# Output projections that finish their token blocks one after another in the last column group

## The chip, the core and the metric

The kernel runs on one core of one Trainium2 chip. The metric is the device time of one execution in microseconds (us), as the median of several executions. A profiled execution also leaves a trace, from which all rows below are taken.

## The reference

The reference is a chain of four transformer-like layers on 256 tokens of width 1024 (plus 256 context tokens in layer 0), all in fp32. What matters here is the same in all four: a mixer (attention in layers 0 and 1, a gated scan in the last two), its output projection into the residual stream through a gate, and a norm that needs whole rows of the updated stream:

```python
x = x + g1 * (mix @ w_out)                 # mix: tokens x 1024, w_out: 1024 x 1024
h = rmsnorm(x, norm2_w) * (1 + sc2) + sh2  # mean of squares over the 1024 columns
x = x + g2 * swiglu(h, ...)                # last layer: eight experts instead
```

Layer 0 does this for 512 tokens (its context rows have a gate of their own), the others for 256.

## The kernel before

The four output projections are calls of `split_linear` (line 746), named `l0_w_out`, `l1_w_out`, and `w_out` for scan layers 0 and 1. They are those calls of it that are given `gates`; each is also given `residual`. The input projections use the same function without either.

The columns of the product are cut into groups (`cols`): two of 512 for an output projection. The tokens are cut into blocks of 128: four in layer 0, two elsewhere. `units[i]` lists the blocks of group i, and each block of a group has its own PSUM bank of 512 fp32 columns. An fp32 product is made of three TensorE products of halves: high by high, high by low, low by high (lines 806, 807, 808). The contraction of 1024 is cut into eight steps k. The order before is: group, then k, then block, so all banks of a group are completed together, in the last k.

The weights of a group come in four pieces of two k each. ScalarE makes the high half of a piece (line 825), VectorE the low half (`lows`, line 844). After the last product of a piece TensorE adds one to `piece_used`. VectorE waits for two pieces of a group and releases the ring slot of its first half, then for all four, releases the second slot, and only then stores the blocks. Each engine runs its own list in order. SyncE's list (`feed`, lines 310 and 316) waits for a released slot and starts the load of the item four places further on in the plan. In the plan an output projection's four half groups are followed by three `ada` items and the first feed-forward weights, in the last layer by the expert weights (`moe`) at once.

A store is two VectorE operations (lines 883 and 884, in layer 0 lines 1718 and 1719): the bank times the gate row into a scratch tile, then the addition to the residual tile. After each store ScalarE squares the new stretch of 512 columns and sums it (`part_square`, line 526).

`with nc.Block()` ends with a barrier of all engines. The next block is `modulate` (line 547): VectorE makes the reciprocal root from the sums (lines 531 and 513 to 518), the two engines normalise the rows (lines 597 and 658), and TensorE meanwhile does one `ada` product (line 420, not in the last layer), spreads gate rows (line 537) and then turns the normalised rows (line 633). The feed-forward block or the router comes after it.

Of the kernel before, what the change touches and what calls it, by code (L numbers as in the profile page):

```python
# [28 lines left out]
KD = D // PB  # L29
# [56 lines left out]
class Signal:  # L86


    def __init__(self, nc, ctx, name):
        self.sem = ctx.enter_context(nc.semaphore(name))  # L90
        self.base = 0
# [14 lines left out]
class Signals:  # L106


    def __init__(self, sig):
        self.ready = sig("ready")  # L110
        self.turned = sig("turned")
        self.evacuated = sig("evacuated")
        self.made = sig("made")
        self.scored = sig("scored")
        self.maxed = sig("maxed")
        self.expd = sig("expd")
        self.p_turned = sig("p_turned")
        self.p_copied = sig("p_copied")
        self.summed = sig("summed")
        self.scaled = sig("scaled")  # L120
        self.kq_turned = sig("kq_turned")
        self.kq_kept = sig("kq_kept")
        self.weighted = sig("probs_weighted")
        self.out_kept = sig("out_kept")
        self.up_done = sig("up_done")
        self.silu_done = sig("silu_done")
        self.act_done = sig("act_done")
        self.hop_a = sig("hop_a")
        self.hop_b = sig("hop_b")
        self.hop_c = sig("hop_c")  # L130
        self.hop_d = sig("hop_d")
        self.down_done = sig("down_done")
        self.hi_gu = sig("hi_gate_up")
        self.hi_d = sig("hi_down")
        self.prod = sig("product_made")
        self.act_hi = sig("hidden_hi")
        self.ada_rows = sig("ada_rows")
        self.ada_kept = sig("ada_kept")
        self.ada_cols = sig("ada_cols")
        self.ada_out = sig("ada_out")  # L140
        self.gate_made = sig("gate_row_made")
        self.gate_kept = sig("gate_row_kept")
        self.ht_kept = sig("turned_kept")
        self.tok_turned, self.tok_hi, self.tok_lo = sig("tokens_turned"), sig("tokens_hi"), sig("tokens_lo")
        self.got_hi, self.got_lo = sig("gathered_hi"), sig("gathered_lo")
        self.hi_kept, self.lo_kept = sig("gathered_hi_kept"), sig("gathered_lo_kept")
        self.lo_kept_act, self.picked = sig("gathered_lo_kept_act"), sig("tokens_picked")
        self.put_turned, self.put_kept = sig("put_turned"), sig("put_kept")
        self.spread, self.spread_kept = sig("gates_spread"), sig("gates_spread_kept")
        self.ht_odd, self.scales = sig("turned_odd_kept"), sig("modulation_scales")  # L150
        self.bank_done, self.tail_added = sig("ffn_bank_done"), sig("ffn_tail_added")
        self.w_hi, self.w_lo = sig("weight_hi"), sig("weight_lo")
        self.h_hi, self.h_lo = sig("input_hi"), sig("input_lo")
        self.piece_used = sig("weight_piece_used")


class MixSignals:
# [55 lines left out]
def build(nc, ctx, d, out):  # L213
# [34 lines left out]
    PS = ctx.enter_context(nc.psum_tensor("ps", [PB, 8, 512], F32))  # L248
# [10 lines left out]
    def sig(name):  # L259
        return Signal(nc, ctx, name)  # L260
# [9 lines left out]
    S = Signals(sig)  # L270
# [100 lines left out]
    def release(eng):  # L371
        eng.sem_inc(front_used.sem, 1)
        eng.sem_inc(back_used.sem, 1)
# [372 lines left out]
    def split_linear(toks, h_hi, h_lo, room, cols, blocks, store, src=None, beside=None, gates=(), nb=0, turned=None,  # L746
# [4 lines left out]
        bank = lambda q: (q % banks + first) % 8  # L751
# [3 lines left out]
        units = [[(b, c0, w) for b in blocks(c0)] for c0, w in cols]  # L755
        starts = [sum(len(u) for u in units[:i]) for i in range(len(units) + 1)]
        total, most = len(units), max(w for _, w in cols)
# [10 lines left out]
        with nc.Block() as block:  # L768
            if beside is not None:
                @block.gpsimd  # L770
                def _(pool):
                    beside(pool)
# [5 lines left out]
            @block.tensor  # L778
            def _(pe):
                if not gates:  # L780
                    zero_products(pe, 8, 7)
                gate_products(pe, gates)
                for k in range(KD if nb else 0):
                    if turn_bank(k) < first:
                        pe.wait_ge(S.gate_kept.sem, S.gate_kept.at(turn_bank(k) // 2 + 1))
                    for b in range(nb):
                        t = pe.transpose(PS[:, turn_bank(k), b * PB:(b + 1) * PB], XN[:, b, k * PB:(k + 1) * PB], ident)
                    t.then_inc(S.turned.sem, 1)
                for i in range(total):
                    for q in range(starts[i], starts[i + 1]):  # L790
                        if q < 8 and bank(q) < first:
                            pe.wait_ge(S.gate_kept.sem, S.gate_kept.at(bank(q) // 2 + 1))
                    if starts[i + 1] > banks:
                        pe.wait_ge(S.evacuated.sem, S.evacuated.at(starts[i + 1] - banks))
                    w = wide(i)
                    for k in range(KD):
                        if k % 2 == 0:
                            pe.wait_ge(S.w_lo.sem, S.w_lo.at(i * per_group + k // 2 + 1))
                        if i == 0:
                            pe.wait_ge(S.h_lo.sem, S.h_lo.at(max(k + 1, len(units[0]) if nb else 0)))  # L800
                        hi = hi_piece(i, k // 2)[:, k % 2 * w:(k % 2 + 1) * w]
                        lo = raw(RINGR, i, k // 2)[:, k % 2 * w:(k % 2 + 1) * w]
                        for j, (b, c0, _) in enumerate(units[i]):
                            o = PS[:, bank(starts[i] + j), 0:w]
                            t = slice(b * PB, (b + 1) * PB)
                            pe.matmul(o, h_hi(k)[:, t], hi, start=(k == 0), stop=False)
                            pe.matmul(o, h_hi(k)[:, t], lo, start=False, stop=False)  # L807
                            mm = pe.matmul(o, h_lo(k)[:, t], hi, start=False, stop=(k == KD - 1))
                        if k % 2 == 1:
                            mm.then_inc(S.piece_used.sem, 1)  # L810
                    if turned and i == 2:
                        turned[0](pe)

# [22 lines left out]
            @block.vector  # L836
            def _(dve):
                def lows(i):
                    for p in range(per_group):
                        if i and p == 2:  # L840
                            dve.wait_ge(S.piece_used.sem, S.piece_used.at((i - 1) * per_group + 2))
                            release(dve)
                        dve.wait_ge(S.w_hi.sem, S.w_hi.at(i * per_group + p + 1))
                        dve.tensor_tensor(raw(RINGR, i, p), raw(flat, i, p), hi_piece(i, p).bitcast(F32),
                                          ALU.subtract).then_inc(S.w_lo.sem, 1)
                        for k in range(2 * p, 2 * p + 2) if i == 0 else ():
                            dve.wait_ge(S.h_hi.sem, S.h_hi.at(k + 1))
                            dve.tensor_tensor(h_lo(k), src(k), h_hi(k).bitcast(F32), ALU.subtract).then_inc(S.h_lo.sem, 1)

                lows(0)  # L850
                if gates:
                    dve.wait_ge(S.gate_kept.sem, S.gate_kept.at(len(gates)))
                for i in range(total):
                    if i + 1 < total:
                        lows(i + 1)
                    else:
                        dve.wait_ge(S.piece_used.sem, S.piece_used.at(i * per_group + 2))
                        release(dve)
                    dve.wait_ge(S.piece_used.sem, S.piece_used.at((i + 1) * per_group))
                    release(dve)  # L860
                    for j, (b, c0, w) in enumerate(units[i]):
                        store(dve, PS[:, bank(starts[i] + j), 0:w], b, c0, w).then_inc(S.evacuated.sem, 1)
        if nb:
            S.turned.done(KD)
        S.gate_made.done(len(gates))
# [8 lines left out]
    def zero_products(pe, n, bank):  # L874

        for _ in range(n):
            pe.matmul(PS[:, bank, :], Z16[:, 0:PB], Z16[:, :], start=True, stop=True)
# [837 lines left out]
    def store_both(dve, ps, b, c0, w):  # L1715
# [9 lines left out]
             gates=[(gate_row, 0, 5, 0), (ctx_gate, 0, 5, 1)])  # L1725
# [446 lines left out]
    for layer in range(2):  # L2172
# [20 lines left out]
        def keep_conv(act):  # L2193
            for j in range(3):
# [12 lines left out]
                 gates=[(gate_row, lay, 5, 2)])  # L2207
        if layer == 0:
# [5 lines left out]
        lg, ix, h1, h2, gates, sel, pos = (SM[:, 32 + 16 * i:48 + 16 * i].rearrange("p (b e) -> p b e", b=2)  # L2214
                                           for i in range(7))
# [380 lines left out]
```

## Time and profile before

| | |
|---|---|
| median of 3 executions | 2720.43 us (2712.69 to 2722.75) |
| the profiled execution | 2713.4 us |
| its span, first to last instruction | 2711.1 us |
| mean granted TensorE clock | 0.953 |
| TensorE matmuls, busy | 2462.7 us (91%) |
| VectorE, busy | 1890.3 us (70%) |
| ScalarE, busy | 1471.5 us (54%) |
| 16 DMA engines' share, mean rate | 674.35 MB at 249 GB/s |

The busy share is a mean over stages that have different limits: the last third of the span is the expert stage. The trace's timelines show each engine's instructions in order of time. A bracket behind a row holds the time that the engine was idle before it, and the instruction that ended the wait. A releaser named PEq L768 is the barrier at the end of a `split_linear` block.

### The profile page before, as it was taken

The page shows a single profiled execution, that of the slowest core. Times are in us where ns is not written, and L with a number is a line of the kernel's source. Part 1 is how long each engine was busy: PE and PEld are TensorE (multiplying, and loading weights), DVE is VectorE, ACT ScalarE, POOL GpSimd, SP SyncE. Part 2 cuts the span into 40 slices and gives each one's busy share as a digit, 9 for nine tenths or more (in the row PEclk, how much of TensorE's full clock was granted, in tenths as well). Part 3 has the DMA queues.
Part 4 walks back from the last instruction along what each step waited for, and adds up shares of the span by engine and source line. Part 5 has one row for each costly group of instructions (what it writes and reads, how often), then busy time and mean ns, then how long its engine had stood idle before and what let it go on. Part 6 is the DMA issues. An engine that isn't in the chain of part 4 may idle for free. (4 is left out here: it accounts for less than half of the span.)

```text
span 2711.1 us, 58120 instructions
## 1 busy us (share of the span) xinstructions
PE 2462.7 (91%) x22998; PEld 1860.1 (69%) x22998; DVE 1890.3 (70%) x2521; ACT 1471.5 (54%) x1865; POOL 14.9 (1%) x12
## 2 busy tenths in 40 slices
PE   6978899999897789999899999888999999999997
PEld 4646677677664457768667768666777777777775
DVE  3276555555645666655666555669999999999997
ACT  3146444433421545443444434348887888888885
POOL 0000000000200000000000000000000000000000
PEclk9989999999888989999799999789999999999999
DMA  7340555554466127545275545338999999999995
GB/s 297 120 191 24 212 203 206 210 200 156 148 227 243 62 99 257 196 177 208 110 260 198 208 157 206 111 138 335 417 414 401 418 418 418 418 408 418 418 416 228
DMA packets 121210, 674.35 MB, mean 249 GB/s; under 512 B 13488, under 2 KB 13968, under 8 KB 67088
## 3 DMA queue, kind: packets, MB, share of 16 engines
q1 hardware_dynamic: 120032, 664.47, 63.6%
q10 hardware_dynamic: 1072, 8.42, 0.9%
q8 instruction: 72, 1.18, 0.2%
q14 instruction: 34, 0.28, 0.0%
HBM read 671.79 MB, written 1.05 MB: 248 GB/s over the span
## 5 line engine op out<-in xcount | busy, mean ns | idle before, releaser
L942 PE MATMUL ps<-projected,normed_or_mix 128*128 128x256 bf16 x1504 | 409.9, 273 | 1.2 <-issue 1.2
L943 PE MATMUL ps<-projected,normed_or_mix 128*128 128x256 bf16 x1504 | 409.9, 273 | 0.0
L1328 DVE TENSOR_TENSOR aux<-weights,aux 128x1024 bf16<-128x1024 f32 x224 | 272.5, 1217 | 2.3 <-ACT aux L1272 2.3
L1323 DVE TENSOR_TENSOR normed_or_mix<-weights,normed_or_mix 128x2048 bf16<-128x2048 f32 x111 | 254.0, 2289 | 15.8 <-ACT normed_or_mix L1266 11.2
L1323 DVE TENSOR_TENSOR turned<-weights,turned 128x2048 bf16<-128x2048 f32 x112 | 256.3, 2289 | 7.3 <-ACT turned L1266 2.6
L1266 ACT ACTIVATE turned<-weights 128x2048 bf16<-128x2048 f32 x112 | 213.6, 1907 | 50.8 <-DMA weights<-moe 50.6
L1266 ACT ACTIVATE normed_or_mix<-weights 128x2048 bf16<-128x2048 f32 x111 | 211.8, 1908 | 49.0 <-DMA weights<-moe 46.2
L1196 PE MATMUL ps<-projected,normed_or_mix 128*128 (+1 forms) x1792 | 234.6, 207 | 3.3 <-DVEq L1353 3.3
L1272 ACT ACTIVATE aux<-weights 128x1024 bf16<-128x1024 f32 x224 | 233.2, 1041 | 3.8 <-PE ps L1210 3.5
L1198 PE MATMUL ps<-projected,normed_or_mix 128*128 (+1 forms) x1792 | 234.6, 207 | 0.0
L1197 PE MATMUL ps<-projected,normed_or_mix 128*128 (+1 forms) x1792 | 234.6, 207 | 0.0
L1196 PE MATMUL ps<-projected,turned 128*128 (+1 forms) x1792 | 233.0, 206 | 0.7 <-DVE turned L1323 0.7
L1198 PE MATMUL ps<-projected,turned 128*128 (+1 forms) x1792 | 233.0, 206 | 0.0
L1197 PE MATMUL ps<-projected,turned 128*128 (+1 forms) x1792 | 233.0, 206 | 0.0
L807 PE MATMUL ps<-weights_halves,normed_or_mix_halves 128*128 128x512 f32 (+4 forms) x576 | 218.6, 379 | 0.0
L1208 PE MATMUL ps<-aux,probs 128*96 128x512 bf16 x448 | 172.6, 385 | 45.9 <-DVE probs L1338 45.9
L944 PE MATMUL ps<-projected,aux 128*128 128x256 bf16 x752 | 205.0, 273 | 0.0
L944 PE MATMUL ps<-projected,normed_or_mix 128*128 128x256 bf16 x752 | 205.0, 273 | 0.0
L974 DVE TENSOR_TENSOR probs_turned<-probs,ps 128x256 f32<-128x256 f32 x94 | 39.6, 421 | 229.3 <-ACT probs L967 229.3
L967 ACT ACTIVATE probs<-ps 128x256 f32<-128x256 f32 x94 | 36.1, 384 | 295.3 <-PE ps L944 295.1
L1196 PEld LDWEIGHTS ps<-projected,normed_or_mix 128*128 128x128 bf16 x1792 | 176.0, 98 | 8.8 <-issue 3.7
L1197 PEld LDWEIGHTS ps<-projected,normed_or_mix 128*128 128x128 bf16 x1792 | 176.0, 98 | 6.5
(385 smaller groups left out, 5960.0 us busy)
## 6 DMA issues: line engine op xcount, KB each, us to landing
weights<-moe SPq DMA_DIRECT2D x224, 1024.0 KB, 8.5
weights<-moe SPq DMA_DIRECT2D x224, 512.0 KB, 6.6
weights<-l_ffn SPq DMA_DIRECT2D x66, 1024.0 KB, 5.1
weights<-ada SPq DMA_DIRECT2D x64, 1024.0 KB, 5.6
weights<-l_ffn SPq DMA_DIRECT2D x66, 512.0 KB, 5.5
weights<-ada SPq DMA_DIRECT2D x64, 512.0 KB, 6.2
weights<-ffn SPq DMA_DIRECT2D x28, 1024.0 KB, 5.2
weights<-w_in SPq DMA_DIRECT2D x24, 948.0 KB, 4.7
```

Source lines behind the costliest of these rows:

```text
L807: pe.matmul(o, h_hi(k)[:, t], lo, start=False, stop=False)
L942: pe.matmul(o, hi, h_hi(k), start=(k == 0), stop=False)
L943: pe.matmul(o, hi, h_lo(k), start=False, stop=False)
L944: mm = pe.matmul(o, lo, h_hi(k), start=False, stop=(k == KD - 1))
L1196: pe.matmul(o, hi[:, t], xh, start=(k == 0), stop=False)
L1197: pe.matmul(o, hi[:, t], xl, start=False, stop=False)
L1198: mm = pe.matmul(o, lo[:, t], xh, start=False, stop=(k == KD - 1))
L1208: pe.matmul(o, hi, w_hi[:, t], start=start, stop=False)
L1266: act.activation(gu4[j % SLOTS][0], RING[:, slot(j), 0:2 * D], ACT.Copy).then_inc(S.hi_gu.sem, 1)
L1272: act.activation(down4[j % SLOTS][0], RING[:, slot(j), 2 * D:3 * D], ACT.Copy).then_inc(S.hi_d.sem, 1)
L1323: dve.tensor_tensor(gu4[j % SLOTS][1], RING[:, slot(j), 0:2 * D], gu4[j % SLOTS][0], ALU.subtract).then_inc(front_used.sem, 1)
L1328: dve.tensor_tensor(down4[j % SLOTS][1], RING[:, slot(j), 2 * D:3 * D], down4[j % SLOTS][0], ALU.subtract).then_inc(back_used.sem, 1)
```

## The change

In the last column group of the calls with `gates`, the block becomes the outer loop and k the inner one: all 24 products of one block, then all 24 of the next. At the end of each block but the last, TensorE signals `block_made`. `piece_used` counts in this group only in the last block. VectorE stores all blocks but the last as their signals come, ahead of its two waits for pieces and its two releases of slots; the last block's store stands behind them, as before. ScalarE's list is not changed. No instruction that computes or loads is added or taken away.

```diff
+        self.block_made = sig("last_group_block")
...
-                    for k in range(KD):
-                        if k % 2 == 0:
+                    last = bool(gates) and i == total - 1
+                    for part, k in itertools.product(range(len(units[i]) if last else 1), range(KD)):
+                        if k % 2 == 0 and part == 0:
                             pe.wait_ge(S.w_lo.sem, S.w_lo.at(i * per_group + k // 2 + 1))
...
                         for j, (b, c0, _) in enumerate(units[i]):
+                            if last and j != part:
+                                continue
...
-                        if k % 2 == 1:
+                        if k % 2 == 1 and (not last or part == len(units[i]) - 1):
                             mm.then_inc(S.piece_used.sem, 1)
+                        elif last and k == KD - 1:
+                            mm.then_inc(S.block_made.sem, 1)
...
+                def keep_block(i, j):
+                    b, c0, w = units[i][j]
+                    store(dve, PS[:, bank(starts[i] + j), 0:w], b, c0, w).then_inc(S.evacuated.sem, 1)
...
                 for i in range(total):
+                    last = len(units[i]) - 1
+                    early = last if gates and i == total - 1 else 0
                     if i + 1 < total:
                         lows(i + 1)
                     else:
+                        for j in range(early):
+                            dve.wait_ge(S.block_made.sem, S.block_made.at(j + 1))
+                            keep_block(i, j)
                         dve.wait_ge(S.piece_used.sem, S.piece_used.at(i * per_group + 2))
                         release(dve)
                     dve.wait_ge(S.piece_used.sem, S.piece_used.at((i + 1) * per_group))
                     release(dve)
-                    for j, (b, c0, w) in enumerate(units[i]):
-                        store(dve, PS[:, bank(starts[i] + j), 0:w], b, c0, w).then_inc(S.evacuated.sem, 1)
+                    for j in range(early, last + 1):
+                        keep_block(i, j)
```

## Rows read from the trace of the kernel before

**Rows 1.** The page's rate of the DMA engines in 40 slices of the span.

```profile
GB/s 297 120 191 24 212 203 206 210 200 156 148 227 243 62 99 257 196 177 208 110 260 198 208 157 206 111 138 335 417 414 401 418 418 418 418 408 418 418 416 228
```

**Rows 2.** Timeline of TensorE, layer 0: start us, duration us, engine, line, operation.

```profile
280.05 0.39 PE L808 MATMUL ps<-projected_halves,turned_halves 128*128 128x512 f32 x1
280.27 0.39 PE L806 MATMUL ps<-projected_halves,normed_or_mix_halves 128*128 128x512 f32 x1
...
280.73 0.39 PE L808 MATMUL ps<-projected_halves,turned_halves 128*128 128x512 f32 x1
...
292.97 0.39 PE L808 MATMUL ps<-projected_halves,turned_halves 128*128 128x512 f32 x1
300.44 2.79 PE L420 MATMUL ps<-weights,silu_cond 128*32 128x384 f32 x16 [7.09 <-PEq L768]
303.16 4.33 PE L537 MATMUL ps<-square_consts,modulations 128*128 128x128 f32 x32
307.33 2.37 PE L633 MATMUL ps<-square_consts,normed_or_mix 128*128 128x128 f32 x20
```

**Rows 3.** Timeline of VectorE, layer 0.

```profile
258.89 4.62 DVE L844 TENSOR_TENSOR weights_halves<-weights,projected_halves 128x1024 fp32r<-128x1024 f32 x4
...
276.55 0.69 DVE L1719 TENSOR_TENSOR ctx_sb<-ctx_sb,aux 128x512 f32<-128x512 f32 x1
293.60 0.69 DVE L1718 TENSOR_TENSOR aux<-ps,gate_rows 128x512 f32<-128x512 f32 x1 [16.35 <-PE ps L808]
...
297.58 0.68 DVE L1718 TENSOR_TENSOR aux<-ps,extra 128x512 f32<-128x512 f32 x1
...
300.29 0.16 DVE L531 SCALAR_TENSOR_TENSOR small<-small 128x4 f32<-128x4 f32 x1 [1.30 <-PEq L768]
```

**Rows 4.** Timeline of ScalarE, layer 0, to the first feed-forward weights.

```profile
299.62 0.19 ACT L526 ACTIVATION_READ_ACCUMULATOR extra<-ctx_sb 128x1 f32 x1
...
304.87 1.14 ACT L597 ACTIVATE normed_or_mix<-ctx_sb,small 128x1024 f32<-128x1024 f32 x1
...
317.56 1.91 ACT L912 ACTIVATE normed_or_mix<-weights 128x2048 bf16<-128x2048 f32 x1
```

**Rows 5.** Timeline of VectorE, layer 1.

```profile
1007.14 0.69 DVE L883 TENSOR_TENSOR aux<-ps,gate_rows 128x512 f32<-128x512 f32 x1 [8.13 <-PE ps L808]
...
1008.47 0.68 DVE L883 TENSOR_TENSOR aux<-ps,gate_rows 128x512 f32<-128x512 f32 x1
```

**Rows 6.** Timeline of TensorE after the projections of layer 1 and the scan layers.

```profile
1006.51 0.39 PE L808 MATMUL ps<-projected_halves,turned_halves 128*128 128x512 f32 x1
1011.32 2.79 PE L420 MATMUL ps<-weights,silu_cond 128*32 128x384 f32 x16 [4.42 <-PEq L768]
1014.04 2.11 PE L537 MATMUL ps<-square_consts,modulations 128*128 128x128 f32 x16
...
1021.08 2.79 PE L480 MATMUL ps<-weights,silu_cond 128*32 128x384 f32 x32
...
1383.44 3.38 PE L537 MATMUL ps<-square_consts,modulations 128*128 128x128 f32 x16
...
1797.31 3.75 PE L537 MATMUL ps<-square_consts,modulations 128*128 128x128 f32 x16 [4.27 <-PEq L768]
```

**Rows 7.** Half-microsecond windows: busy by engine, PEclk, DMA share, GB/s.

```profile
297.00:297.50 0.50, 0.00 (x0) 0.00 (x0) 0.50 (x1) 0.15 (x2) 0.00 (x0) 0.89 1.01 393
...
1010.50:1011.00 0.50, 0.00 (x0) 0.00 (x0) 0.00 (x0) 0.20 (x2) 0.00 (x0) 0.77 1.00 401
...
1379.00:1379.50 0.50, 0.00 (x0) 0.00 (x0) 0.29 (x1) 0.12 (x1) 0.00 (x0) 0.91 1.05 442
...
1795.50:1796.00 0.50, 0.00 (x0) 0.00 (x0) 0.50 (x1) 0.01 (x1) 0.00 (x0) 0.84 0.93 393
```

**Rows 8.** Timeline of SyncE's queue, layer 0: the starts of loads.

```profile
282.56 0.33 SPq L310 DMA_DIRECT2D weights<-ada  x1
...
293.83 0.42 SPq L316 DMA_DIRECT2D weights<-l_ffn  x1
```

More of the change, by code:

```diff
@@ L860, in _ @@
                     release(dve)
-                    for j, (b, c0, w) in enumerate(units[i]):
-                        store(dve, PS[:, bank(starts[i] + j), 0:w], b, c0, w).then_inc(S.evacuated.sem, 1)
+                    for j in range(early, last + 1):
+                        keep_block(i, j)
+        if gates:
+            S.block_made.done(len(units[-1]) - 1)
         if nb:
```

## The prediction

> **What bounds the kernel now.** I read the page first, then the timelines of the engines around each of the four output projections. The page's rate row [rows 1] splits the span: some 830 us at the end run near 418 GB/s and are fed by memory, everything before it is not. All four projections lie before that stretch, so what counts there is the chain of engines.
>
> In layer 0 TensorE is dense up to its last product, which starts at 292.97 and ends at 293.36 us, and then waits 7.09 us for the barrier [rows 2]. VectorE had waited 16.35 us for that last product, because all four banks come ready together; then it runs eight operations in a row [rows 3], and ScalarE follows it with four squares and ends at 299.62 + 0.19 = 299.81 [rows 4]. Nothing else is under way but loads. So the tail of a projection, last product to barrier, is a chain on which only VectorE and then ScalarE work, and it is on the path. Layer 1 shows the same with two blocks: VectorE waits 8.13 us, stores twice [rows 5], and TensorE starts again after 4.42 us [rows 6]. The scan layers repeat layer 1's pattern; the last of them has 4.27 us [rows 6].
>
> **The change, part by part.**
>
> *TensorE's order.* The number of products stays. Three products belong to one block and one k. From the last product of one block to the first of the next, which goes to another bank, it is 280.27 - 280.05 = 0.22 us; inside the three, in one bank, two steps take 280.73 - 280.27 = 0.46, 0.23 each [rows 2]. So the trace sees no price for staying in a bank nor for leaving it. The stationary halves change as often as before. One block of 24 products then takes 24 x 0.227 = 5.4 us. I take 0 for the new order. The bounds: below, 0, since the engine has no gap that could close here; above, if a product had to wait for the end of the one before it in its bank, 0.39 in place of 0.23 each; that is a rival below.
>
> *Low halves of the weights.* The first block now wants all four pieces within its own 5.4 us, not within the whole group. In layer 0 the last is made at 258.89 + 4.62 = 263.51 [rows 3] and the last group starts four blocks before 293.36, at 271.6. In the two-block layers VectorE finishes the pieces as the first group ends, and the fourth is wanted three quarters of a block (4.1 us) later. Cost 0; if that cover were gone each microsecond late would count once.
>
> *Stores moved.* In layer 0 the blocks are complete at about 277.0, 282.5, 287.9 and 293.4. VectorE finishes the first group's stores at 276.55 + 0.69 = 277.24 [rows 3], so it is free for the first block at once, and one store, 1.33 us, is a quarter of a block. Three of four stores move from the tail to beside the products. Each also carries ScalarE's square with it, which starts when its addition is done and takes 0.8. The tail shortens by 297.58 - 293.60 = 3.98 us [rows 3]: the fourth store's start moves to where the first one's was. In each of the other three it shortens by 1008.47 - 1007.14 = 1.33 us [rows 5]. Sum: 3.98 + 3 x 1.33 = 7.97 us. What is late next is the one store that is left, its square, and the barrier.
>
> *Waits added.* VectorE waits for `block_made` up to three times. Behind these waits stand only stores and the releases. The release of the first slot of the last group moves from the middle of the group to the middle of its last block: in layer 0 from 282.5 to 290.6, elsewhere by 2.7 us. SyncE's two loads behind it (from 282.56 [rows 8]) move with it, and now run into the pair that starts with the last release; that pair ends its issue at 293.83 + 0.42 = 294.25 [rows 8], before the new end of the tail (the first store's start at 293.60 plus what now follows the fourth's, 299.81 - 297.58 = 2.23, is 295.83), so SyncE does not hold up the barrier. The two items together are 3 MB, some 7.5 us at the 400 GB/s of such windows [rows 7], so both have landed by about 301. The first reader of the later one is the cast at 317.56 [rows 4], which moves to about 313. That leaves 12 us. Cost 0. In the last layer the item held back is the third of the expert weights, wanted some 40 us later. If the cover were gone, the lateness of a cast would be paid once a layer.
>
> *What starts earlier.* After the barrier everything hangs on it: `modulate`, then the feed-forward block, whose loads are released by its own casts, or the router and then the expert stage. The latter is fed by memory, but its stream of 220 loads beyond the first four waits for the first release of the router block, so it starts earlier by as much. I therefore keep the whole 7.97.
>
> *TensorE's clock.* In all four tails the granted clock falls from the upper level (2.4 GHz) to the lower (1.2 GHz) while the engine is idle: at 297.4, 1010.8, 1379.4 and 1795.8, from the shares in their windows [rows 7], which is 4.0, 3.9, 3.1 and 2.8 us after its last product. The 16 `ada` products then take 2.79 us, against half of 2.79 for 32 of the same size at the upper level (at 1021.08 [rows 6]), 1.40: 1.39 lost, three times, 4.2 in all. Spreading the gate rows takes 3.38 and 3.75 us in the scan layers against at most 2.11 in layer 1 [rows 6], another 1.3 + 1.6. Upper bound 7.1 us, if no tail loses the clock. With the change TensorE waits 7.1 - 4.0 = 3.1 us in layer 0, as long in the next two and 4.27 - 1.33 = 2.9 in the last. Two of the four falls came later after the last product than that, one together with it and one before. From two tails kept, 2.8 us; but ScalarE's copy of the normalised rows, which must be ready before they are turned, ends at 306.01 in layer 0, little before the turns at 307.33 [rows 2, 4], and gives part of it back. Lower bound 0 (a loss would want a longer gap, and none is made). I take half of the two tails' 2.8: 1.4 us.
>
> The Trainium skill (page "TensorE: Matmul & The Clock Gate", section "What's actually happening") says that the monitor behind the clock runs freely and does not start with the kernel, so the same kernel meets it at another phase each time. By it the moments of the four falls are luck of this execution; the scatter from 2.8 to 4.0 us agrees. It is why I count a half and not the two tails in full; the sum by the two tails in full would be 10.8.
>
> **Sum.** 7.97 + 1.4 = 9.4 us. The profiled execution of 2713.4 us would take 2704.0. It lies 7.0 us under the median of the three executions, 2720.43; the change has nothing to do with what scatters them, so the median would be 2711.0, 0.35% less.
>
> **Rivals.**
>
> *The clock stays up in all tails.* For it: the new gap is as short as one of the falls and shorter than two. Against it: one fall came after 2.8 us. Gain 7.97 + 7.1 = 15.1, time 2705.3.
>
> *Given back or hidden anyway.* The ordered loads now collide, or the barrier was waiting for something else. For it: two items are released close together, and the expert stage lasts as long as its bytes do. Against it: 12 us of room, and a tail in which no engine but these two works. If it holds in full the time is 2720.4; if for layer 0's larger part only, the gain is 4 + 1.4 and the time 2715.0.
>
> *The change doesn't do what it says.* VectorE's list could hold the early stores back. Against it: in front of them stand only the first group's stores, which end at 277.24, 0.2 us after the first block. A late start by that much moves nothing, as 4.1 us of idle time follow each store. It is part of the case before.
>
> *One bank is slow (the other side).* 24 products in a row add into one bank. If each had to see the end of the one before, 0.39 us apart and not 0.23, the last groups' 96 + 3 x 48 = 240 products would cost 240 x 0.16 = 38 us more, less the 9.4: 2749. It decides from 9.4 / 240 = 0.04 us per product. For it only that the trace has no longer run than three products in a bank here; against it the equal steps in and between banks [rows 2].
>
> **How the numbers follow.** Chances: the forecast 0.72, the clock up in all tails 0.13, given back wholly or in part 0.12, the slow bank 0.03. The range takes in the forecast with a clock term from 0 to 7.1 (2712.5 to 2705.3), the scatter of single executions of 10 us, halved for a median, on either side, and the partial loss; I give 2702 to 2719. Less than 2 in 10 is outside: the slow bank and the ends of the scatter. A measurement of this kernel can tell about 0.5% from no change, 13.6 us. Only the second rival passes that (0.13), and the forecast where the scatter of medians helps it, about one time in seven (0.10): faster 0.23. The forecast's rest and the loss: same 0.74. Slower 0.03.
>
> **What would show it.** Right: in the last group of layer 0 three pairs of stores 5.4 us apart beside the products, one pair after the last; TensorE's wait at the barrier of 2.9 to 3.1 us in all four tails; `L420` at 1.4 us where the windows show the upper clock, 2.79 where not; loads of the last group's first slot 8 us later, and no wait of the cast at line 912 for a DMA. Wrong: steps in the last group over 0.23 us; a store starting later than 0.3 us after its block; a barrier that waits for SyncE; or the gain of a tail missing again at the start of the feed-forward or the expert stage behind it.

## The result, and the profile after

| comparison | changed kernel, median (range) | before, median (range) | ratio, 95% interval |
|---|---|---|---|
| first | 2701.64 us (2699.58 to 2705.24), 4 runs | 2720.90 us (2712.69 to 2722.75), 4 runs | 0.9934 [0.9917, 0.9951] |
| `again` | 2706.83 us (2698.37 to 2713.50), 6 runs | 2717.77 us, 24 runs | 0.9950 [0.9932, 0.9969] |
| `again_b` | 2706.61 us (2698.28 to 2711.80), 6 runs | 2718.55 us, 22 runs | 0.9948 [0.9929, 0.9968] |
| `again_c` | 2704.38 us (2700.68 to 2710.66), 6 runs | 2718.17 us, 11 runs | 0.9951 [0.9935, 0.9967] |

The change makes the kernel faster. The first comparison rests on four executions of each kernel; over all four the medians are 2705.2 us (22 executions) and 2718.2 us (61), 13.0 us or 0.48% less. The forecast was 9.4 us. Its time, 2711.0 us with a range of 2702 to 2719, lies above all four medians: the first falls 0.4 us below the range, the other three lie inside it.

The profiled execution of the changed kernel took 2701.12 us (span 2698.8). Its TensorE timeline in layer 0, the answer to [rows 2] (start, duration, engine, line; lines 810, 811, 812, 421, 538 and 634 are 806, 807, 808, 420, 537 and 633 of before):

```profile
276.63 0.39 PE L812 MATMUL ps<-projected_halves,turned_halves 128*128 128x512 f32 x1
276.85 0.39 PE L810 MATMUL ps<-projected_halves,normed_or_mix_halves 128*128 128x512 f32 x1
...
277.31 0.39 PE L812 MATMUL ps<-projected_halves,turned_halves 128*128 128x512 f32 x1
...
294.31 0.39 PE L812 MATMUL ps<-projected_halves,turned_halves 128*128 128x512 f32 x1
297.80 1.50 PE L421 MATMUL ps<-weights,silu_cond 128*32 128x384 f32 x16 [3.11 <-PEq L769]
299.23 3.84 PE L538 MATMUL ps<-square_consts,modulations 128*128 128x128 f32 x32
302.90 2.37 PE L634 MATMUL ps<-square_consts,normed_or_mix 128*128 128x128 f32 x20
```

Its VectorE timeline there, for [rows 3]: the first operation of each store of the last group, and the barrier.

```profile
278.51 0.68 DVE L1735 TENSOR_TENSOR aux<-ps,gate_rows 128x512 f32<-128x512 f32 x1
...
283.85 0.69 DVE L1735 TENSOR_TENSOR aux<-ps,gate_rows 128x512 f32<-128x512 f32 x1 [3.94 <-PE ps L812]
...
289.29 0.69 DVE L1735 TENSOR_TENSOR aux<-ps,extra 128x512 f32<-128x512 f32 x1 [4.02 <-PE ps L812]
...
294.94 0.69 DVE L1735 TENSOR_TENSOR aux<-ps,extra 128x512 f32<-128x512 f32 x1 [4.23 <-PE ps L812]
...
297.65 0.16 DVE L532 SCALAR_TENSOR_TENSOR small<-small 128x4 f32<-128x4 f32 x1 [1.30 <-PEq L769]
```

It shows three stores beside the products and one behind them, and a wait of TensorE of 3.11 us where it was 7.09. All of this projection starts 1.34 us later than in the execution of before (its first group's first store at 273.19 against 271.85), and the block behind the barrier starts 2.64 us earlier: 3.98 between the two. The 16 `ada` products take 1.50 us and not 2.79, the clock having stayed up (granted share 1.00 from 298 to 303 us).

The layer 1 tail, for [rows 6], TensorE and the windows of the clock (busy by engine, PEclk, DMA share, GB/s):

```profile
1004.45 0.39 PE L812 MATMUL ps<-projected_halves,turned_halves 128*128 128x512 f32 x1
1007.94 1.68 PE L421 MATMUL ps<-weights,silu_cond 128*32 128x384 f32 x16 [3.10 <-PEq L769]
1009.56 3.46 PE L538 MATMUL ps<-square_consts,modulations 128*128 128x128 f32 x16
1012.85 0.82 PE L634 MATMUL ps<-square_consts,normed_or_mix 128*128 128x128 f32 x6
```

```profile
1008.50:1009.00 0.50, 0.50 (x12) 0.16 (x4) 0.40 (x4) 0.00 (x0) 0.00 (x0) 1.00 1.04 442
1009.00:1009.50 0.50, 0.50 (x8) 0.00 (x0) 0.43 (x3) 0.00 (x0) 0.00 (x0) 0.63 0.89 377
```

Here the wait is shorter too (3.10 against 4.42), but the clock falls all the same, at 1009.1, when TensorE has been at work again for 1.2 us (0.8 to 1.2 in the four profiled executions of the changed kernel). So the `ada` products keep most of their speed and the gate rows lose theirs: 3.46 us where they took 2.11.

In scan layer 0 the fall still comes during the wait, and the `ada` products are slow as before. What is gained is the gate rows, 2.20 us where [rows 6] has 3.38:

```profile
1374.70 2.79 PE L421 MATMUL ps<-weights,silu_cond 128*32 128x384 f32 x16 [3.10 <-PEq L769]
1377.42 2.20 PE L538 MATMUL ps<-square_consts,modulations 128*128 128x128 f32 x16
```

The clock is up again 3.1 us after the restart here and 5.5 us after it in the kernel before; in scan layer 1 it is 3.0 and 5.4.

The loads of the last group's first slot, SyncE's queue and the first cast of the feed-forward weights (line 929, 912 of before), for [rows 8] and [rows 4]:

```profile
292.06 0.33 SPq L311 DMA_DIRECT2D weights<-ada  x1
292.82 0.33 SPq L317 DMA_DIRECT2D weights<-ada  x1
294.78 0.33 SPq L311 DMA_DIRECT2D weights<-l_ffn  x1
295.17 0.42 SPq L317 DMA_DIRECT2D weights<-l_ffn  x1
```

```profile
313.14 1.90 ACT L929 ACTIVATE normed_or_mix<-weights 128x2048 bf16<-128x2048 f32 x1
```

The first load stands 9.50 us later than before, 8.2 of it the moved release and 1.3 the later start of this projection. The cast has no bracket: it did not wait.

The difference of the two profiled executions, 12.3 us of span, can be read stage by stage from such rows. A tail runs from the end of a projection's last product to TensorE's first instruction behind the barrier that is not an idle product; a modulation from there to TensorE's first instruction of the block after it. The last two rows run from VectorE's first operation of the modulation that leads into the scan layer to the last product of its output projection. Times in us, each column one profiled execution (the four of the changed kernel as a range):

| stage | before | changed (4) | `order_only` | `before_warm` | `after_warm_b` | `all_warm` |
|---|---|---|---|---|---|---|
| tail, layer 0 | 7.08 | 3.10-3.11 | 7.08 | 7.09 | 3.11 | 3.10 |
| tail, layer 1 | 4.42 | 3.10-3.13 | 4.45 | 4.46 | 3.10 | 3.10 |
| tail, scan 0 | 4.41 | 3.09-3.10 | 4.42 | 4.42 | 3.09 | 3.12 |
| tail, scan 1 | 4.28 | 2.94-2.95 | 4.28 | 4.27 | 2.95 | 2.95 |
| modulation, layer 0 | 12.60 | 11.02-11.03, once 12.54 | 13.81 | 11.02 | 11.02 | 11.03 |
| modulation, layer 1 | 8.81 | 9.26-9.28 | 9.09 | 7.67 | 7.67 | 7.67 |
| modulation, scan 0 | 10.08 | 9.05-9.12 | 10.29 | 7.67 | 7.80 | 7.68 |
| modulation, scan 1 | 7.43 | 6.94 | 7.43 | 7.57 | 6.93 | 6.93 |
| scan 0, mixer and projection | 173.05 | 171.19-171.48 | 173.10 | 171.51 | 171.95 | 169.92 |
| scan 1, mixer and projection | 172.13 | 171.06-171.12 | 172.15 | 171.15 | 172.26 | 171.67 |

The tails give 7.96 us, the modulations behind them 2.56 in the first profiled execution, and the two mixers of the scan layers another 2.58: 13.1 together, against 13.0 by the medians of all executions. The kernel before has one profiled execution only; `order_only`, whose tails are as long, shows how far such a column repeats: its layer 0 modulation is 1.2 us longer, its mixers agree within 0.05. The stages that are left differ by some us in either direction from execution to execution of one kernel: the expert stage took 896.1, 899.7, 900.1 and 896.5 us in the four, and layer 1's mixer 327.9, 328.4, 331.7 and 325.2.

### The profile page after: what moved, and what is told of

Its sections match the earlier page's. It is cut to its first block and busy times, and to the rows that moved or that the text cites. A ratio compares the mean times of both kernels' runs of the same rounds, so it can differ in the third digit from the quotient of the medians.

```text
span 2698.8 us, 58018 instructions
## 1 busy us (share of the span) xinstructions
PE 2443.1 (91%) x22896; PEld 1854.2 (69%) x22998; DVE 1892.0 (70%) x2521; ACT 1472.7 (55%) x1865; POOL 14.9 (1%) x12
```

## The experiments

Twelve runs of nine kernels, in three sets; within a set all ran on one chip beside the kernel before.

### The whole change again, and its parts

> The changed kernel once more, so that it stands beside the others on one chip. Theory (stores leave the tail, 7.97 us; TensorE's clock falls less often or for less time, 0 to 7 us; the rest is scatter): 8 to 15 us faster than before, ratio 0.9945 to 0.997. Rival (the first comparison's 18 us are the change's own doing): 16 us or more, ratio 0.994 or less.

Measured 0.9950 [0.9932, 0.9969], 13.6 us. It lies in the theory's span. The rival's 0.994 is excluded by none of the three intervals, though the next two give 0.9948 and 0.9951; what speaks against it is the sum of 13.1 us read from the stages above.

`order_only`: TensorE's new order, the stores as before.

```diff
-                    early = last if gates and i == total - 1 else 0
+                    early = 0
```

> TensorE's order of the changed kernel, all stores after the last product as before. Theory: no price and no gain of the order, 0 us within 3; products in the last group 0.227 us apart. Rival (the order itself is faster or slower, a bank's price): a step of the last groups' 240 products that differs from 0.227 by 0.01 would be 2.4 us, and all of the 18 us would want 0.07 less.

Measured 1.0006 [0.9995, 1.0017], +1.6 us (-1.4 to +4.6): the order alone gives nothing that can be told from zero. Its products in the last group of layer 0, all into one bank:

```profile
288.37 0.39 PE L810 MATMUL ps<-projected_halves,normed_or_mix_halves 128*128 128x512 f32 x1
288.60 0.39 PE L811 MATMUL ps<-weights_halves,normed_or_mix_halves 128*128 128x512 f32 x1
288.83 0.39 PE L812 MATMUL ps<-projected_halves,turned_halves 128*128 128x512 f32 x1
289.05 0.39 PE L810 MATMUL ps<-projected_halves,normed_or_mix_halves 128*128 128x512 f32 x1
```

Three steps take 0.68 us, as in [rows 2]. The slow bank is out.

`layer0_only` and `others_only`: the change only where a group has four blocks, or only where it has two.

```diff
-                    last = bool(gates) and i == total - 1
+                    last = bool(gates) and len(units[i]) == 4 and i == total - 1    # 2 in others_only
...
-                    early = last if gates and i == total - 1 else 0
+                    early = last if gates and last == 3 and i == total - 1 else 0   # 1 in others_only
```

> The change in layer 0's output projection alone (four blocks). Theory: 3.98 us from the tail and up to 2 from TensorE's clock in the modulation behind it: 4 to 6 us. Rival (the gain is not the tails'): another share than 4 in 8.

> The change in the three output projections of two blocks. Theory: 3 x 1.33 = 4.0 us and 0 to 5 from the clock: 4 to 9 us. With layer0_only the two gains should add up to that of the whole change.

Measured 0.9979 [0.9970, 0.9987], 5.7 us (3.5 to 8.2), and 0.9965 [0.9953, 0.9977], 9.5 us (6.3 to 12.8). Together 15.2, against 13.6 of the whole. Three stores that left layer 0's tail bring 5.7 us; three others, one in each of the other tails, bring 9.5 although they save the same 4.0 directly. So some 5.5 us of these (2.3 to 8.8) come from elsewhere than the stores; the 9.5 lie just above the 4 to 9 expected.

The two traces show where. The mixers of the scan layers took 173.02 and 172.12 us in `layer0_only`, as before, and 171.45 and 171.09 in `others_only`, as in the whole change. The stages of `others_only` give 4.0 us for the tails, 1.0 for the modulations behind them and 2.6 for the mixers: 7.6 us, inside its interval.

### What the gain over the stores is

`refilled`: idle work of VectorE in the tail, in the place and at the price of the stores that moved.

```diff
+                    for _ in range(early):
+                        u = AUX[:, 3072:3584]
+                        dve_step(dve, dve.tensor_tensor(u, u, GB[:, 0:512], ALU.mult))
+                        dve_step(dve, dve.tensor_tensor(u, u, GB[:, 0:512], ALU.add))
                     for j in range(early, last + 1):
                         keep_block(i, j)
```

> The changed kernel, but VectorE does idle work of the price of the stores that moved (two operations of 512 columns for each) between the last product and the last store, so that the tail is as long as before while the order, the early stores and the later release stay. Theory (all of the gain is the shorter tail, directly or by the shorter wait of TensorE): time as before, within 2 us. Rival (the order, the early squares or the later loads bring a share): it stays faster than before by that share, 4 us or more.

Measured 0.9998 [0.9984, 1.0012], 0.5 us (-3.3 to 4.3). Its tails are back at 7.46, 4.56, 4.55 and 4.40 us, and the clock's loss is back with them:

```profile
1015.42 2.79 PE L421 MATMUL ps<-weights,silu_cond 128*32 128x384 f32 x16 [4.56 <-PEq L769]
1018.13 2.23 PE L538 MATMUL ps<-square_consts,modulations 128*128 128x128 f32 x16
```

Order, early squares and later loads are thus worth nothing by themselves that this comparison can see (within some 4 us); the gain comes with the length of the tail.

`before_warm` (the kernel before) and `after_warm` (the changed one): products of zeros into a bank that was stored a group ago, so that TensorE works while it would wait.

```diff
                     if turned and i == 2:
                         turned[0](pe)
+                if gates:
+                    pe.wait_ge(S.evacuated.sem, S.evacuated.at(starts[1]))
+                    zero_products(pe, 30 if len(units[0]) == 4 else 18, bank(0))    # 12 in after_warm
```

> The kernel before, with idle products (128x512, zeros, 30 in layer 0, 18 elsewhere) behind each output projection's last product, so that TensorE works through the tail. It measures the clock's share alone. Theory: the upper clock stays through all tails, the 16 products of the modulation take 1.4 and not 2.8 us, gain 4 to 7 us and nothing more. Rival (the clock's share is small): 0 to 2 us. A loss would mean that the idle products delay the barrier.

> The changed kernel with 12 such idle products behind each output projection's last one. Theory: the tails of the changed kernel that still lose the clock keep it, 1 to 4 us faster than the changed kernel, and faster than both kernels. Rival (the shorter wait has already given all of it): same as the changed kernel.

`before_warm`: 0.9966 [0.9954, 0.9978], 9.2 us (6.0 to 12.5) with the stores where they were. Its layer 1 tail:

```profile
1008.70 3.83 PE L880 MATMUL ps<-zeros_bf 128*128 128x512 bf16 x17
1013.09 1.50 PE L420 MATMUL ps<-weights,silu_cond 128*32 128x384 f32 x16 [0.56 <-PEq L768]
1014.51 2.05 PE L537 MATMUL ps<-square_consts,modulations 128*128 128x128 f32 x16
1016.48 0.87 PE L633 MATMUL ps<-square_consts,normed_or_mix 128*128 128x128 f32 x6
```

Same tail as before (4.46 us in the table), a granted share of 1.00 through it and through the 16 products, and the modulation 7.67 us where it was 8.81. (The kernel issues 18 idle products here; 17 stand in the row.) The four modulations together give 5.0 us, and the mixers of the scan layers 2.5 on top, though nothing in them was touched. The 9.2 are more than the 4 to 7 expected, "and nothing more" did not hold, and the clock alone is worth about as much as the stores.

`after_warm`: 0.9936 [0.9920, 0.9953] beside `again_b` with 0.9948 [0.9929, 0.9968]. Medians 2700.54 and 2706.61 us: 6 us faster by them, 3 by the ratios, whose intervals overlap. It was run once more.

### How far the clock reaches

`ffn_warm` puts 20 idle products behind the last one of each dense feed-forward block, whose own tail is 4.94 us long. `all_warm` has these and the 12 of `after_warm`.

```diff
             def _(pe):
                 products(pe)
+                zero_products(pe, 20, 5)
```

> The changed kernel as the neighbour of the next three, on their chip: as in its other runs, 10 to 15 us faster than before.

> The changed kernel with idle products behind the output projections, once more: 2 to 6 us faster than the changed kernel, if the first comparison was not scatter.

> The changed kernel with 20 idle products behind the last product of each of the four dense feed-forward blocks, none behind the output projections. Theory (the clock is also lost in the waits behind these blocks, and what a tail does to it is handed on through the dense block to the wait behind it): the clock stays up behind them, the modulation of the next layer is shorter by 1 to 2 us each, 3 to 7 us faster than the changed kernel. Rival (only the projections' tails matter): same as the changed kernel.

> Idle products behind the output projections and behind the feed-forward blocks. Theory: both gains add, 5 to 11 us faster than the changed kernel and the fastest of all. Rival (they share the same clock loss): no faster than the better of the two.

| kernel | median | ratio to before |
|---|---|---|
| `again_c` | 2704.38 us | 0.9951 [0.9935, 0.9967] |
| `after_warm_b` | 2698.12 us | 0.9924 [0.9906, 0.9941] |
| `ffn_warm` | 2703.39 us | 0.9941 [0.9923, 0.9958] |
| `all_warm` | 2694.50 us | 0.9906 [0.9888, 0.9924] |

`after_warm_b` repeats: 6.3 us by the medians, 7.3 by the ratios, whose intervals again overlap a little (0.9941 and 0.9935). Its trace does not show where they come from. Against the changed kernel its modulations are 2.9 us shorter by the table, its scan mixers 1.8 us longer, and the feed-forward block between them 0.95 longer (226.06 us against 225.11; 226.03 in `after_warm`). That leaves some 0.2 us, so this gain is measured twice and not explained.

`ffn_warm` is inconclusive, 1.0 us by the medians and 2.7 by the ratios, less than the 3 expected. Its stages have 2.8 us of gain, 2.2 of them in layer 0's feed-forward block, which has a wait in its middle (361.3 us against 363.3 to 363.7). `all_warm` is 9.9 us faster than `again_c`, and its interval ends where that of the changed kernel has not begun (0.9924 against 0.9935). It is the fastest of all, 23.7 us below the kernel before; its stages show some 6 of the 9.9 us. That it beats `after_warm_b` (3.6 us by medians) is likely and not shown.

TensorE's first instructions of the modulation that leads into scan layer 0 show what it adds. Before, changed and `all_warm` in turn:

```profile
1203.40 5.35 PE L420 MATMUL ps<-weights,silu_cond 128*32 128x384 f32 x32 [4.94 <-PEq L1144]
```

```profile
1200.28 4.45 PE L421 MATMUL ps<-weights,silu_cond 128*32 128x384 f32 x32 [4.94 <-PEq L1161]
```

```profile
1193.21 4.48 PE L897 MATMUL ps<-zeros_bf 128*128 128x512 bf16 x20
1198.31 2.79 PE L421 MATMUL ps<-weights,silu_cond 128*32 128x384 f32 x32 [0.62 <-PEq L1164]
```

The same 32 products take 5.35, 4.45 and 2.79 us. Between the first two nothing differs at this place, not even the wait; what differs is the clock. These are the windows of the 32 products, before and changed (the third value from the end is the granted share):

```profile
1203.40:1208.75 5.35, 5.35 (x33) 1.66 (x34) 2.63 (x14) 1.53 (x2) 0.00 (x0) 0.50 0.76 238
```

```profile
1200.28:1204.73 4.45, 4.45 (x32) 1.47 (x32) 2.63 (x14) 1.45 (x2) 0.00 (x0) 0.62 0.72 227
```

The other traces fall on the same two sides: 5.35 us in `layer0_only`, 4.42 and 4.43 in `others_only` and `before_warm`.

## Why the prediction was right, and where it was not

- **The tail.** Right in mechanism and size. Expected 3.98 + 3 x 1.33 = 7.97 us, 7.96 read from the table; waits of 2.9 to 3.1 us expected, 2.94 to 3.13 found in all sixteen tails of four executions.
- **The order.** Priced at 0; shown by `order_only`. The rival of the slow bank is refuted.
- **Low halves, release, loads.** Priced at 0. The loads moved by 8.2 us as worked out, and the cast did not wait; `refilled` keeps all of these moves and equals the kernel before.
- **Given back.** Refuted: the parts add up to the whole, and the expert stage starts 11.7 us earlier in the profiled execution (VectorE's first operation of it at 1826.31 against 1837.98).
- **The clock.** This is the term that was mis-sized: "I take half of the two tails' 2.8: 1.4 us". Measured, the gain over the stores is 13.0 - 8.0 = 5.0 us. The clock's whole share, stores untouched, is 9.2 (6.0 to 12.5) against an "upper bound" of 7.1, which the interval does not exclude. Two steps in it failed.
 First, the tails were chosen by when the clock had fallen in one execution, layers 0 and 1. Layer 0 did keep it, in three executions of four (1.6 us). Layer 1 did not: the clock falls 1.2 us after the restart instead of during the wait, and its modulation is 0.46 us longer than before (0.2 to 0.3 longer than in `order_only` and `layer0_only`, with 9.09 and 8.96 us). So the reason given for the lower bound, that a loss would want a longer gap, does not hold either. The two scan layers, given nothing, brought 0.96 and 0.49 us, because there the clock was up again earlier after the restart. A fall need not come while the engine is idle.
 Second, the bound counted only the instructions right behind the four tails. There it was too high: with the clock up in all four, `before_warm` gained 5.0 us and not 7.1. Beyond them it counted nothing. The two scan mixers, a whole feed-forward block later, became 1.6 to 1.9 and 1.0 us shorter in the four executions of the changed kernel, in `before_warm` and in `others_only`, and not in `order_only` or `layer0_only`. That they follow the clock and not the stores is shown by `before_warm`. The shift can go the other way too: in `after_warm_b` the second of them took 172.26 us, as before. How it is handed on is argued only: between layer 1's modulation and the first mixer lies a block of constant length (182.91 to 182.92 us in the four), so a changed moment of the rise in front of it can change the moment of the next fall behind it. The windows fit: from the rise in layer 1 to the next fall it is 187.7 us in both kernels (1014.2 to 1201.9 before, 1012.5 to 1200.3 changed).
- **Luck of the execution.** By the Trainium skill (page "TensorE: Matmul & The Clock Gate", section "What's actually happening") I took the moments of the falls for luck, since the monitor runs freely. Layer 0 bears it out (a modulation of 11.03 us three times and 12.54 once). Behind it the measurement says otherwise: the modulations of layer 1 and the scan layers agree within 0.07 us over four executions. The long tails were no luck there either. In the traces of the kernel before, `order_only` and `layer0_only` the fall comes 3.8 to 4.1 us after the last product in layer 1, 3.1 in scan layer 0 and 2.8 in scan layer 1. So the half that was taken for luck stood for something that repeats.
- **The time.** 2711.0 was forecast; 2701.6 was measured first and 2704.4 to 2706.8 in the later comparisons. Against the median of all executions, 2705.2, the forecast is 5.8 us too high: 3.6 by the clock's term and 2.2 by the base, since 2720.43 was the median of three executions and all 61 have 2718.2. The first comparison's 19.3 us, by its medians, are more than the change gives; the rest is the scatter of four executions, as the changed kernel's own span 15 us. Sign and mechanism were right, "same" within 0.5% was given 0.74, and the change is on that line (0.48% over all, 0.66% at first).

## What to carry to other kernels

Where a barrier follows a matrix product, let the accumulators finish one by one, so that all but the last are stored beside products; the gain is the stores' time in the tail, and it can be read from one timeline. Then look at what the wait does to TensorE's clock: here the change gained 5 us by it on top of the stores' 8, and a dozen idle products in the wait made the kernel some 6 us faster in two comparisons, by a way that the traces do not show. Price the clock by the whole program up to the next barriers, not by the instructions behind one wait.

## What the runs showed of the hardware

A wait cut from 4.4 to 3.1 us can leave the clock's loss about as large as it was and only move it: layer 1 lost 1.3 us on its gate rows and won 1.1 on its `ada` products. Idle products of zeros kept the granted clock up (share 1.00, 16 products in 1.50 us behind 18 of zeros, 2.79 behind a wait). A shift of the clock showed again behind the next wait, a dense block of 182.9 us later: at equal code and an equal wait of 4.94 us the 32 products behind took 5.35 us or 4.45.
